# Even-layer differential attention: halves of the scores in three PSUM slots in turn, transposes and outputs in the fourth, first maxima ahead of combinations

## The reference, cut to what matters

```python
def diff_attn_core(q, k, v, lam):
    s = jnp.einsum('bqhmd,bkhmd->bhmqk', q, k).astype(F32) * (B_HEAD_DIM ** -0.5)
    p = jax.nn.softmax(s, axis=-1)
    a = p[:, :, 0] - lam * p[:, :, 1]
    return jnp.einsum('bhqk,bkhd->bqhd', a.astype(v.dtype), v)

ob_l = sweep_query_blocks(lambda qb: diff_attn_core(qb, k_all, v_all, lam), q_l)   # 512 queries, 768 keys
ob_c = diff_attn_core(q_c, k_c, v_c, lam)                                          # 256 queries, 256 keys
```

## Time and profile before

| | |
|---|---|
| median of three executions | 1701.07 us |
| the profiled execution, its time | 1700.79 us |
| its span | 1699.1 us |
| mean granted TensorE clock | 0.979 |
| PE busy | 1559.6 us, 92% |
| DVE busy | 905.6 us, 53% |
| ACT busy | 520.0 us, 31% |
| POOL busy | 156.3 us, 9% |
| first scores of the attention start | 330.95 us |
| ACT's last copy of transposes starts | 442.50 us |

### The profile page before, as it was taken

One profiled execution on the slowest core, in us unless ns is written; L12 is line 12 of the kernel. 1 busy time (PEld: TensorE's weight loads), 2 busy tenths in 40 slices (PEclk: granted clock), 3 DMA queues, 4 the chain that ended last, 5 costly groups with the idle time before them and its releaser, 6 DMA issues.

```text
span 1699.1 us, 22727 instructions
## 1 busy us (share of the span) xinstructions
PE 1559.6 (92%) x8470; PEld 1073.2 (63%) x8470; DVE 905.6 (53%) x1571; ACT 520.0 (31%) x836; POOL 156.3 (9%) x203
## 2 busy tenths in 40 slices
PE   5799999789899989999999989899999898898985
PEld 2588888668788868778788867785343333333441
DVE  2676536666557845566789788777222112121124
ACT  3412222367424345455351367313000000000011
POOL 2000010022300100000222040200000000000003
PEclk8999999979999999999999999999999999999998
DMA  9222355200322321043434202249999999999995
GB/s 377 115 99 100 114 191 202 83 14 13 131 111 87 125 87 50 18 169 122 151 144 149 100 13 89 86 198 382 406 423 422 423 422 423 423 422 422 422 379 206
DMA packets 57620, 353.08 MB, mean 208 GB/s; under 512 B 7376, under 2 KB 7632, under 8 KB 20544
## 3 DMA queue, kind: packets, MB, share of 16 engines
q1 hardware_dynamic: 43200, 307.41, 45.2%
q0 software_dynamic: 9248, 35.63, 5.7%
q10 hardware_dynamic: 5088, 8.92, 1.4%
HBM read 332.53 MB, written 23.59 MB: 210 GB/s over the span
## 4 chain that ended last, share of the span: by engine, by line
PE 61%; DMA 14%; DVE 11%; ACT 5%; issue 4%; SPq 3%; POOL 1%; DVEq 0%; ACTq 0%; POOLq 0%
PE ps L2264 10%; PE ps L2265 10%; PE ps L2266 10%; DMA early<-in_experts 10%; PE ps L2816 7%; PE ps L2305 4%; PE ps L2836 4%; SPq L705 3%; PE ps L2774 3%; PE ps L2479 3%; PE ps L2503 2%; ACT p L993 1%; PE ps L2496 1%; DMA early<-in_ada 1%; PE ps L2216 1%
## 5 line engine op out<-in xcount | busy, mean ns | idle before, releaser
L2264 PE MATMUL ps<-whi,xth 128*128 128x512 f32 (+1 forms) x768 | 301.1, 392 | 13.3 <-DVE xtl L1391 8.9
L2265 PE MATMUL ps<-wlo,xth 128*128 128x512 f32 (+1 forms) x768 | 297.0, 387 | 0.0
L2266 PE MATMUL ps<-whi,xtl 128*128 128x512 f32 (+1 forms) x768 | 296.9, 387 | 0.0
L2816 PE MATMUL ps<-early,xe_t 128*64 128x512 f32 x904 | 207.6, 598 | 31.1 <-DMA early<-in_experts 25.4
L2264 PEld LDWEIGHTS ps<-whi,xth 128*128 128x128 f32 x768 | 145.1, 189 | 45.1 <-DVE xtl L1391 6.4
L2816 PEld LDWEIGHTS ps<-early,xe_t 128*64 128x64 f32 x904 | 60.8, 136 | 172.0 <-issue 104.6
L2266 PEld LDWEIGHTS ps<-whi,xtl 128*128 128x128 f32 x768 | 145.1, 189 | 29.7
L2265 PEld LDWEIGHTS ps<-wlo,xth 128*128 128x128 f32 x768 | 145.3, 189 | 27.6
L2098 DVE TENSOR_TENSOR hid<-hid,ps 128x256 f32<-128x256 f32 x33 | 13.9, 421 | 251.5 <-ACT hid L1279 251.5
L1335 DVE TENSOR_TENSOR wlo<-raw,whi 128x2048 fp32r<-128x2048 f32 (+3 forms) x52 | 103.1, 1984 | 67.0 <-ACT whi L911 66.3
L1279 ACT ACTIVATE hid<-ps 128x256 f32<-128x256 f32 x33 | 12.7, 384 | 391.9 <-PE ps L2816 391.9
(11 more groups left out here) (463 smaller groups left out, 2700.6 us busy)
## 6 DMA issues: line engine op xcount, KB each, us to landing
early<-in_experts SPq DMA_DIRECT2D x128, 1024.0 KB, 26.4
raw<-in_experts SPq DMA_DIRECT2D x51, 1024.0 KB, 25.2
raw<-in_ada SPq DMA_DIRECT2D x40, 1024.0 KB, 6.7
ring<-in_experts SPq DMA_DIRECT2D x15, 1024.0 KB, 27.7
raw<-in_even SPq DMA_DIRECT2D x14, 1024.0 KB, 5.5
raw<-in_second SPq DMA_DIRECT2D x10, 1024.0 KB, 5.0
early<-in_ada SPq DMA_DIRECT2D x8, 1024.0 KB, 18.2
pair_dram<-tmp ACTq DMA_DIRECT2D x60, 128.0 KB, 6.7
```

The costliest lines, as they stand in the source:

```text
L2264: nc.tensor.matmul(v, a[0], b[0], start=first, stop=False)
L2265: nc.tensor.matmul(v, a[0], b[1], start=False, stop=False)
L2266: return nc.tensor.matmul(v, a[1], b[0], start=False, stop=last)
L2816: mm = nc.tensor.matmul(ps[SLOT * t:SLOT * t + SLOT, 4 + s, :], xe_t[:, 2 * i + k, SLOT * s:SLOT * s + SLOT], w[:, D * k + 512 * t:D * k + ...
```

## The change

- **Slots.** The halves of all units take slots 0, 1, 2 in turn, by their number 2 u + i modulo 3. T(u) always takes slot 3. O(u) has no job of its own: it is written to columns 768 to 895 of slot 3 (`unit_out`), behind the transposes' 768 columns, in the second of the slot's two banks. Two semaphores guard it: `s_unit_out` (PE has written) and `s_unit_kept` (ACT has read). The transposes 4 and 5 of a latent unit write to that bank, so PE waits for `s_unit_kept` ahead of transpose 4. After the attention the turn of slots goes on at 0; before, it went on at 1.
- **PE.** Unit u: S(u+2, 0), T(u), S(u+2, 1), O(u). The filler products go to the slot of S(22, 1).
- **ACT.** Unit u: copy of T(u), second exponential of u + 1, first exponential of u + 2, output.
- **DVE.** Unit u: first maximum of u + 1, combination u, second maximum of u + 1. At the start the first maximum of unit 1 stands ahead of combination 0, and its second one behind `qk_low(2)`.
- **Semaphores.** Two new ones are made, and four of the odd layer (`s_kr_hi`, `s_kr_lo`, `s_qr_hi`, `s_qr_lo`) become `s_rot_hi` and `s_rot_lo`, with the counts of the waits moved up by one. The order of the work there is the same; those hunks are left out below.

```diff
-    for u in range(2):
-        plan.job("S", "even", u, 0)
-        plan.job("S", "even", u, 1)
+    for n in range(4):
+        plan.job("S", "even", n // 2, n % 2, slot=n % 3)
     for u in range(E_UNITS):
-        plan.job("T", "even", u)
         if u + 2 < E_UNITS:
-            plan.job("S", "even", u + 2, 0)
-            plan.job("S", "even", u + 2, 1)
-        plan.job("O", "even", u)
+            plan.job("S", "even", u + 2, 0, slot=(2 * u + 4) % 3)
+        plan.job("T", "even", u, slot=3)
+        if u + 2 < E_UNITS:
+            plan.job("S", "even", u + 2, 1, slot=(2 * u + 5) % 3)
+    plan.next = 0
...
+        unit_out = slot_at(3)[:, TOK:TOK + P]
...
-            def exps(u):
-                m = u // 4
-                for i, pbuf in ((0, p0[:, u % 3, 0:keys(m)]), (1, p1[:, u % 2, 0:keys(m)])):
-                    if i == 0 and u >= 3:
-                        filled(act, "T", "even", u - 3)
-                    if i == 1 and u >= 2:
-                        act.wait_ge(s_comb, u - 1)
-                    act.wait_ge(s_nb, 2 * u + i + 1)
-                    st = soft[:, u % 4, :]
-                    own(nc.scalar.activation(pbuf, slot(("S", "even", u, i))[:, 0:keys(m)], ACT.Exp,
-                                         bias=st[:, 2 + i:3 + i],
+            def exp(u, i):
+                n = keys(u // 4)
+                pbuf = (p0[:, u % 3, 0:n], p1[:, u % 2, 0:n])[i]
+                if i == 0 and u >= 3:
+                    filled(act, "T", "even", u - 3)
+                if i == 1 and u >= 2:
+                    act.wait_ge(s_comb, u - 1)
+                act.wait_ge(s_nb, 2 * u + i + 1)
+                st = soft[:, u % 4, :]
+                own(nc.scalar.activation(pbuf, slot(("S", "even", u, i))[:, 0:n], ACT.Exp, bias=st[:, 2 + i:3 + i],
                                          accum_out=st[:, 4 + i:5 + i]), ev("S", "even", u, i))
 
             nc.scalar.preload_act_table(ACT.Exp)
             qk_high(1)
-            exps(0)
+            exp(0, 0)
+            exp(0, 1)
             qk_high(2)
-            exps(1)
+            exp(1, 0)
             qk_high(3)
             for u in range(E_UNITS):
                 v = filled(act, "T", "even", u)
                 if u >= 2:
-                    filled(act, "O", "even", u - 2)
+                    act.wait_ge(s_unit_out, u - 1)
                 n = keys(u // 4)
                 own(nc.scalar.activation(pt[:, u % 2, 0:n], v[:, 0:n], ACT.Copy), ev("T", "even", u))
                 if u == E_UNITS - 1:
                     split_high(plan.through["eout", "p"] - 1)
+                if u + 1 < E_UNITS:
+                    exp(u + 1, 1)
                 if u + 2 < E_UNITS:
-                    exps(u + 2)
-                v = filled(act, "O", "even", u)
+                    exp(u + 2, 0)
+                act.wait_ge(s_unit_out, u + 1)
                 o = o_rows[:, u // 4, P * (u % 4):P * (u % 4) + P]
-                own(nc.scalar.activation(o, v[:, 0:P], ACT.Copy, scale=soft[:, u % 4, 6:7]), ev("O", "even", u))
+                own(nc.scalar.activation(o, unit_out, ACT.Copy, scale=soft[:, u % 4, 6:7]), s_unit_kept)
                 own.free(nc.scalar.activation(junk[:, P * (u % 4):P * (u % 4) + P], o, ACT.Square,
                                               accum_out=oss[:, u:u + 1]), s_oss)
...
-            def maxima(u):
+            def maxi(u, i):
                 st = soft[:, u % 4, :]
-                n = keys(u // 4)
-                for i in range(2):
-                    v = filled(dve, "S", "even", u, i)
-                    own(nc.vector.tensor_reduce(st[:, 2 + i:3 + i], v[:, 0:n], AX, ALU.max, negate=True), s_nb)
+                v = filled(dve, "S", "even", u, i)
+                own(nc.vector.tensor_reduce(st[:, 2 + i:3 + i], v[:, 0:keys(u // 4)], AX, ALU.max, negate=True), s_nb)
 
             def combine(u):
 
@@ -1519,23 +1522,26 @@
                 evacuated(dve, "S", "even", u, 0)
                 evacuated(dve, "S", "even", u, 1)
                 if u >= 4:
-                    evacuated(dve, "O", "even", u - 4)
+                    dve.wait_ge(s_unit_kept, u - 3)
                 own(nc.vector.reciprocal(st[:, 6:8], st[:, 4:6]))
                 own(nc.vector.scalar_tensor_tensor(st[:, 7:8], st[:, 7:8], nlam, st[:, 4:5], ALU.mult, ALU.mult))
                 own(nc.vector.scalar_tensor_tensor(p0[:, u % 3, 0:n], p1[:, u % 2, 0:n], st[:, 7:8], p0[:, u % 3, 0:n],
                                                    ALU.mult, ALU.add), s_comb)
 
-            maxima(0)
+            maxi(0, 0)
+            maxi(0, 1)
             qk_low(1)
+            maxi(1, 0)
             combine(0)
             qk_low(2)
-            maxima(1)
+            maxi(1, 1)
             qk_low(3)
-            for u in range(E_UNITS):
+            for u in range(1, E_UNITS):
                 if u + 1 < E_UNITS:
-                    combine(u + 1)
-                if u + 2 < E_UNITS:
-                    maxima(u + 2)
+                    maxi(u + 1, 0)
+                combine(u)
+                if u + 1 < E_UNITS:
+                    maxi(u + 1, 1)
...
-            def scores(u):
+            def scores(u, i):
                 m, h = u // 4, u % 4
                 if m == 0:
                     pe.wait_ge(s_qk_lo, 2 * h + 2)
                 at_ = slice(P * m, P * m + P)
-                for i in range(2):
-                    f = slice(64 * i, 64 * i + 64)
-                    v = begin("S", "even", u, i)
-                    for lo in range(0, keys(m), 512):
-                        hi = min(lo + 512, keys(m))
-                        mm = three(v[:, lo:hi], (qt_h[f, h, at_], qt_l[f, h, at_]), (kt_h[f, h, lo:hi], kt_l[f, h, lo:hi]),
-                                   True, True)
-                    end(mm, "S", "even", u, i)
-
-            scores(0)
-            scores(1)
+                f = slice(64 * i, 64 * i + 64)
+                v = begin("S", "even", u, i)
+                for lo in range(0, keys(m), 512):
+                    hi = min(lo + 512, keys(m))
+                    mm = three(v[:, lo:hi], (qt_h[f, h, at_], qt_l[f, h, at_]), (kt_h[f, h, lo:hi], kt_l[f, h, lo:hi]),
+                               True, True)
+                end(mm, "S", "even", u, i)
+
+            for n in range(4):
+                scores(n // 2, n % 2)
             for u in range(E_UNITS):
                 m, h = u // 4, u % 4
+                if u + 2 < E_UNITS:
+                    scores(u + 2, 0)
                 pe.wait_ge(s_comb, u + 1)
-                turn(("T", "even", u), [p0[:, u % 3, P * n:P * n + P] for n in range(keys(m) // P)],
-                     [P * n for n in range(keys(m) // P)])
+                v = begin("T", "even", u)
+                for n in range(keys(m) // P):
+                    if n == 4:
+                        pe.wait_ge(s_unit_kept, u)
+                    mm = nc.tensor.transpose(v[:, P * n:P * n + P], p0[:, u % 3, P * n:P * n + P], ident[:])
+                end(mm, "T", "even", u)
                 if u + 2 < E_UNITS:
-                    scores(u + 2)
+                    scores(u + 2, 1)
                 if u == E_UNITS - 2:
-                    occupy_next(2, "O", "even", u)
-                v = begin("O", "even", u)
+                    occupy(2, slot(("S", "even", u, 1))[:, 0:512])
+                if u:
+                    pe.wait_ge(s_unit_kept, u)
                 evacuated(pe, "T", "even", u)
                 last = keys(m) // P - 1
                 for n in range(last + 1):
-                    mm = nc.tensor.matmul(v[:, 0:P], pt[:, u % 2, P * n:P * n + P], vb[:, n, P * h:P * h + P],
+                    mm = nc.tensor.matmul(unit_out, pt[:, u % 2, P * n:P * n + P], vb[:, n, P * h:P * h + P],
                                           start=n == 0, stop=n == last)
-                end(mm, "O", "even", u)
+                mm.then_inc(s_unit_out, 1)
```

More of the change, by code:

```diff
@@ L554, in build @@
         s_nbo, s_oy = sem("s_nbo"), sem("s_oy")
-        s_kr_hi, s_kr_lo, s_q_hi, s_qr_hi, s_qr_lo = (sem(n) for n in ("s_kr_hi", "s_kr_lo", "s_q_hi", "s_qr_hi", "s_qr_lo"))
+        s_q_hi, s_rot_hi, s_rot_lo = (sem(n) for n in ("s_q_hi", "s_rot_hi", "s_rot_lo"))
+        s_unit_out, s_unit_kept = sem("s_unit_out"), sem("s_unit_kept")
         s_hr, s_h2, s_fw, s_first = sem("s_hr"), sem("s_h2"), sem("s_fw"), sem("s_first")
@@ L1099, in _ @@
                     act.wait_ge(s_kr, 1)
-                    own.free(nc.scalar.activation(kr_h[:], kr_t[:], ACT.Copy), s_kr_hi)
+                    own.free(nc.scalar.activation(kr_h[:], kr_t[:], ACT.Copy), s_rot_hi)
                 for f in range(4):
@@ L1105, in _ @@
                     act.wait_ge(s_qr, 2 * g + j + 1)
-                    own.free(nc.scalar.activation(qr_h[:, j, :], tmp[:, j, 0:SEQ], ACT.Copy), s_qr_hi)
+                    own.free(nc.scalar.activation(qr_h[:, j, :], tmp[:, j, 0:SEQ], ACT.Copy), s_rot_hi)
                 for m in range(NT):
@@ L1684, in _ @@
```

(11 more changed lines are left out.)

## The result

The changed kernel took **1717.41 us** (median of four, 1717.22 to 1721.2) beside 1701.13 us before (four, 1699.31 to 1704.82): ratio **1.0089, interval 1.0067 to 1.0112**. The forecast was 1704.4, its range ended at 1707.5, and the result is slower by more than the forecast said. The profile shown here is of the execution of 1721.2 us, the longest of the four; that of before is of 1700.79 us.

The account below looks back on a forecast made before the run. PE, at 4.79 us a latent unit over 4.55 for DVE and ACT, was taken to become the bound. Start +1.9, transposes 1 to combination 22 +3.2, tail -1.6 gave +3.5 us: 1704.4 us, range 1698.5 to 1707.5.

Parts of the forecast that it names:

- transposes 1 to combination 22: Main stretch of the even layer's attention: 93.6 us against 90.4 before, +3.2 us, with the clock rising at the same work.
- two mixed units: Two units between context and latent ones: 3.5 us each at full clock, 7.0 us together.
- the start: Attention up to transposes 1: first scores wait for slot 0, transposes 0 stand behind scores 2; 346.8 against 344.91, +1.9 us.
- the tail: End of combination 22 to ACT's last copy: 5.55 us against 7.17 before, -1.6 us.
- Rival 3: The clock rises late, dense scores being broken up by transposes: 1.5 to 3 us more, 1707 us; chance 0.10.
- an early rise: Second rival: PE without idle in the context units gets 2.4 GHz from unit 2 or 3 on; 1700.5 us, chance 0.13.
- PE order in the latent units: PE's new order gives a 4.79 us loop, over DVE and ACT's 4.55, so PE binds; -0.4 us over 14 units.
- Rival 1: PE doesn't bind; the shorter loop of DVE and ACT sets the pace: -3.5 us, 1697.3 us; chance 0.13.
- Context units: Eight 256-key units at low clock: halves can't overlap, so 3.65 us a unit on PE against 2.81 before.
- my 0.09: Cost in us at full clock of each switch into or out of the 64-row form on PE, from odd-layer rows.
- Reordered maxima: Latent units: loop left on DVE and ACT is 4.55 us against 4.82; alone worth 3.8 us.
- At nothing: Parts priced at zero: merged semaphores, shifted later slots, the wait ahead of transposes 4 and 5, SP's queue, POOL's loads.

Follow-up runs that it names:

- the padded kernel: Changed kernel with queries zero-padded so scores run on 128 rows from block 1 on, that block's padding made in two parts: 1700.36 us, ratio 0.9974.

## Why the prediction was wrong

**The step that failed** is one sentence of the part on transposes 1 to combination 22: "I let the clock rise at the same point of the work, once 512-column scores run." It didn't: 512-column scores run from 363.48 on (before: 360.73, with the clock up at 363), and the clock stayed at the 1.2 GHz level to about 394. I forecast 93.6 us from transposes 1 to the end of combination 22; it was 452.67 - 346.21 = 106.5, 12.9 more. By pieces: to the end of combination 8 29.5 against 26.5 (+3.0: two mixed units at the low clock); combinations 8 to 11 23.65 against 3 x 4.79 (+9.3: the low clock); 11 to 21 48.84 against 47.9 (+0.9); the last one 4.48 against 4.79 (-0.3). With the start 0.6 and the tail 0.1 us better than forecast, the stage ends 12.1 us later than my 3.5, at 15.6. What the late rise goes with is shown: the 64-row scores, for padded to 128 rows in the same order they let the clock rise at about 352. What it is about them stays open.

**Rival 3 named what happened**, a late rise, with a chance of 0.10 and a price of 1.5 to 3 us. Its reason, dense scores broken up by transposes, isn't enough: the padded kernel keeps that order and its clock rises at about 352; and with paired halves on the new slots it rose only near 383. The price was about 12 (3.0 + 9.3), because I bounded the rise by a few units' worth of work where nothing in the trace bounded it. The rows had a warning that I used for the opposite end only: PE was busy 2.81 of 3 us at 0.50, which I read as evidence against an early rise. It said as much about a late one: busy time alone doesn't bring the clock up in this stage. The clock should have been priced over the whole stretch, each latent unit at the low clock costing 3.9 us more.

**Right**, step by step:
- *PE order in the latent units*: 4.82 at full clock, forecast 4.79. PE bound, without idle (48.98 of 49.00 us). Rival 1 (PE doesn't bind) is out. The transposes are 4.85 us apart on the mean from 398 to 447, 4.82 in most units and 4.90 in every fourth. They start 0.40 us behind the combination, where I had named 0.1 to 0.3.
- *Context units*: 3.64, forecast 3.65. Here, as in the latent units, the sum held but not its parts, which is luck: at full clock the padded kernel has the scores 0.62 us behind the first transpose in place of 0.81, and 1.33 behind the first output product in place of 1.53, so going into the 64-row form costs about 0.2 us, more than my 0.09. Leaving it costs less: ahead of the outputs nothing (0.21 us behind the last score product, 406.41 to 406.62, against 0.22 in the padded kernel, 396.63 to 396.85), and a whole half takes 1.24 us with the change of form (403.33 to 404.57) and 1.23 without (395.62 to 396.85, padded). The totals came out since the 0.09 that I charged for leaving is there without any change of form, and since the rows of before that I took for the transposes held a way in already.
- *Start*: +1.3 (346.21 against 344.91), forecast +1.9. The evacuations ahead began 0.54 us earlier in this profile (329.31); counted from them it is +1.8. First scores 333.39, forecast 333.9. *Tail*: 5.44, forecast 5.55.
- *Reordered maxima*: the shorter loop of DVE and ACT that I priced at 4.55 is real. It is 4.47 in the padded kernel, where nothing hides it. In the change PE covers it, as forecast.
- *At nothing*: no wait for the last output's copy ahead of transposes 4 and 5 stands on the chain shown. Of the 4.8 us behind the stage by which the two profiles differ, part is clock: both profiles of the changed kernel have it low for some 3 us near 575 and near 654, that of before hasn't. That isn't the merged semaphores' doing, for the kernel before with fillers in the middle has such places near 563 and 643.

PE was busy 20.00 of 20 us at 0.50 (374 to 394). By the Trainium skill, page "TensorE: Matmul & The Clock Gate", section "Part 1: The HAM clock gate", the gate follows how busy PE has been, and activity releases it; the traces here don't agree where the busy time is of this form.

## What to carry to other kernels

Busy time of PE alone doesn't bring its clock up: look at PEclk in each stretch, and where products on part of the rows run alone or alternate with full ones, price the stretch at both levels in full. Zero-padding a 64-row product to 128 rows cost no time on PE where it couldn't be paired with its other half anyway (1.23 us a half against 1.24); it saved 0.8 us of changes of form a unit at the low clock, let the clock rise some 40 us earlier, and turned a loss of 0.9% into a gain of 0.26%. Padding the kernel before, whose halves are paired, was not tried. A reordering that shortens one loop (here DVE and ACT's, to 4.47 us) pays only once the next engine's loop has been brought below it.

## What the runs showed of the hardware

- With lone 64-row products between 128-row ones, PE was granted 1.2 GHz for about 60 us (332 to 394) though it was busy without a break for the last 48 of them. In two profiles of it, the rise came at 394 and 392. The same kernel started at full clock by fillers fell back within the context units, at about 347.
- With score products on 128 rows the clock rose at about 345 (scores of both halves) and 352 (zero-padded, in time), and held at a PE that was busy 77% (12.27 of 16 us).
- One added 64-row product of 256 columns a half moved the rise from about 352 to 370 in the slowest of ten executions; five of the ten had a mean granted clock as high as without it (0.980 to 0.983).
- The moment of the rise isn't fixed in the kernel before: about 363 in one profile, 378 in another with fillers at the start only. Its executions on other chips had a mean granted clock of 0.968 to 0.980; a comparison of single executions can be off by several microseconds for this reason.
- Going into the 64-row form costs about 0.2 us of PE at full clock (0.81 - 0.62, 1.53 - 1.33); the four changes of form cost 0.8 us a unit at half clock (3.64 - 2.83), 0.65 of it on the two ways in.
- The small DVE operation ahead of the combination, 0.22 us, took 0.65 us in every fourth latent unit of the changed kernel and 1.01 to 1.09 in the padded one. It then ends with an operation of GpSimd, within 0.02 us: 407.72 + 0.65 against 407.08 + 1.28 in the changed kernel, whose timeline has

```profile
407.72 0.65 DVE L1527 SCALAR_TENSOR_TENSOR stat<-stat 128x1 f32<-128x1 f32 x1
```

```profile
407.08 1.28 POOL L782 TENSOR_TENSOR o_rows<-o_rows,z_in 128x512 f32<-128x512 f32 x1
```

It costs under 0.1 us while PE's loop is the longer one (transposes 4.91 us apart in place of 4.82), and 0.8 us every fourth unit in the padded kernel.
